# One HGRN2 / forgetting-attention / MoE step: the HGRN rows of w_out multiplied inside decode, the other rows later, by tokens

## The chip, the core and the metric

The kernel runs on one NeuronCore of a Trainium2 chip, in float32 throughout. The time is device microseconds of one execution. The kernel before took 1868.43 us (median of 3 runs, 1866.72 to 1868.97).
## The reference, cut to what matters

```python
def merge_heads(fox_o, hgrn_o, hg, mem_o, g_hn, w_out):
    hgrn_o = rms_norm(hgrn_o, g_hn).reshape(B, L, HGRN_W) * jax.nn.silu(hg)
    cat = concatenate([fox_o (6*128), hgrn_o (6*128), mem_o (4*128)], axis=-1)
    return cat @ w_out                       # w_out 2048 x 2048

# prompt: 256 tokens; sample: 8 batches x 4 tokens, each over 1024 paged keys (8 pages) + 4 new
fox_o = fox_attend(fq, k_all, v_all, c_q, c_k, ...)   # 6 heads
mem_o = memory_attend(mq, mk, mv)                     # 4 heads, 256 memory tokens
h = x + merge_heads(...)
y = h + hier_moe(rms_norm(h), ...)    # group logits (4), expert logits (32), top-2, 32 experts of 512
```

Prompt and sample tokens together are T = 288 (tiles of 128, 128 and 32). The sample's attention (decode) reads per batch 8 key pages and 8 value pages of 384 KB and 512 KB each of memory keys and values. The experts' weights are 403 MB.

## The kernel before

All engines run programs written out by hand in one block; semaphores alone order them. The span has four stages.

1. **Projections, prompt attention, HGRN2** (0 to 583 us), not touched by the change.
2. **Decode** (583 to 752 us). Per batch, TensorE transposes the keys in 14 units of four 128x128 blocks (`key_in`, L2044; 12 units of pages, 2 of memory keys) into PSUM banks, ACT copies the even units out and DVE the odd ones (`key_out`, L1062 and L1447). Four banks (0 to 3) take turns. `decode_scores` (L2061 to L2073) makes scores, maximum and exponential go over ACT and DVE, `probs_in` transposes the probabilities, `decode_values` (L2104 to L2111) multiplies with the value pages, `decode_heads` (L2119, L2120) picks the heads. TensorE's order is a pipeline over batches: the units of batch b+1 are transposed in the loop of batch b, with that batch's small steps between them, then values(b), scores(b+1), heads(b). Value pages lie in two sets of 8 (POOL issues them, one set refilled after each `decode_values`); key pages in one set, each reloaded by SP once its unit is transposed.
3. **w_out and router** (752 to 905 us). For each of 16 blocks of 128 output columns, 16 products with the w_out block [128x128] stationary and `cat` [128x288] moving (L2172) give the block with columns on partitions. ACT copies it, TensorE transposes it back to tokens (`by_token`, L2147), DVE adds it to `h_tok` (L1523), which x was loaded into; TensorE transposes `h_tok` again (`block_transposed`, L2156), DVE multiplies with the norm's gain, `block_logits` (L2161) makes the 36 logits with tokens in the free dimension; at the end three transposes (L2186) turn them. ACT sums squares (L1100). SP loads w_out in 8 slabs of 2 MB into a ring of 3, and x and the router's weights `w_rt` before slab 3.
4. **MoE** (from 905 us). DVE chooses experts (L1541 on), TensorE gathers tokens (L2203) and multiplies four experts side by side, each in 32 columns of the array (L2239, L2280). Eight units of 2 MB of the first pair of groups are loaded ahead; the ring proper starts with the first unit used (`units_used`, SP L659), so it moves with the gather.

## Time and profile before

| | us |
|---|---|
| median of 3 runs | 1868.43 |
| profiled execution, first to last instruction (span) | 1862.4 |
| median less span (what lies around it) | 6.0 |
| DVE ends the gate product (L1437), the last work ahead of decode | 587.95 |
| first `decode_values` | 615.97 |
| last `decode_values` | 742.03 |
| first product of w_out | 752.04 |
| first logits added by DVE (L1541) | 905.36 |
| first gather (L2203) | 915.43 |

The record gives the profiled execution its span alone, so it is set against the median by the difference of the two, 6.0 us. TensorE (PE) is busy 80% of the span, the 16 DMA engines nearly all of the last 940 us. A stage must be read by itself: the rows further down give busy time, TensorE's granted clock (1.00 is 2.4 GHz, 0.50 is 1.2 GHz), DMA share and GB/s of each.

### The profile page before, as it was taken

The page shows a single profiled execution, that of the slowest core. Times are in us where ns is not written, and L with a number is a line of the kernel's source. Part 1 is how long each engine was busy: PE and PEld are TensorE (multiplying, and loading weights), DVE is VectorE, ACT ScalarE, POOL GpSimd, SP SyncE. Part 2 cuts the span into 40 slices and gives each one's busy share as a digit, 9 for nine tenths or more (in the row PEclk, how much of TensorE's full clock was granted, in tenths as well). Part 3 has the DMA queues.
Part 4 walks back from the last instruction along what each step waited for, and adds up shares of the span by engine and source line. Part 5 has one row for each costly group of instructions (what it writes and reads, how often), then busy time and mean ns, then how long its engine had stood idle before and what let it go on. Part 6 is the DMA issues. An engine that isn't in the chain of part 4 may idle for free.

```text
span 1862.4 us, 23477 instructions
## 1 busy us (share of the span) xinstructions
PE 1485.4 (80%) x9493; PEld 884.7 (48%) x9493; DVE 438.5 (24%) x1140; ACT 219.5 (12%) x508; POOL 78.8 (4%) x141
## 2 busy tenths in 40 slices
PE   6999999999998899999867576576765666666746
PEld 5777777776776666777532131221312213122211
DVE  3106664542133333011301101002010020110201
ACT  3000101003323333111300000000000000000000
POOL 1000000220002221000000000000000000000000
PEclk9999999999999999999887788788888887777878
DMA  7444243432444998636399999999999999999996
GB/s 249 131 131 134 69 137 133 133 126 68 132 156 172 370 396 308 211 118 247 160 414 427 428 427 429 428 429 429 429 429 428 429 428 428 428 429 429 427 427 224
DMA packets 130315, 555.09 MB, mean 298 GB/s; under 512 B 13827, under 2 KB 83524, under 8 KB 104836
## 3 DMA queue, kind: packets, MB, share of 16 engines
q1 hardware_dynamic: 121972, 517.82, 69.9%
q0 software_dynamic: 8272, 36.25, 5.4%
q8 instruction: 53, 0.87, 0.2%
q14 instruction: 18, 0.15, 0.0%
HBM read 545.32 MB, written 8.72 MB: 297 GB/s over the span
## 4 chain that ended last, share of the span: by engine, by line
PE 65%; DMA 29%; DVE 3%; SPq 1%; issue 1%; ACT 1%; DVEq 0%; ACTq 0%
PE PS L1720 21%; PE PS L2239 16%; DMA arena<-in_w_up_e_dram 9%; DMA arena<-in_w_down_e_dram 8%; DMA arena<-in_w_gate_e_dram 8%; PE PS L2280 7%; PE PS L2172 7%; DMA arena<-in_cache_mem_k_dram 3%; PE PS L2044 1%; PE PS L1759 1%; PE PS L2104 1%; PE PS L2203 1%; SPq L669 1%; PE PS L2061 1%; PE PS L1811 1%
## 5 line engine op out<-in xcount | busy, mean ns | idle before, releaser
L1720 PE MATMUL PS<-arena 128*128 128x288 f32 (+1 forms) x1728 | 445.2, 407 | 3.0 <-DVE arena L1191 1.1
L2239 PE MATMUL PS<-arena 128*32 128x512 f32 x1792 | 288.7, 727 | 199.0 <-DMA arena<-in_w_up_e_dram 129.7
L1720 PEld LDWEIGHTS PS<-arena 128*128 128x128 f32 x1728 | 322.3, 191 | 96.3 <-issue 20.3
L2239 PEld LDWEIGHTS PS<-arena 128*32 128x32 f32 x1792 | 69.8, 131 | 409.5 <-issue 194.3
L2280 PE MATMUL PS<-arena 128*32 128x512 f32 x872 | 141.4, 731 | 113.9 <-DMA arena<-in_w_down_e_dram 113.9
L2239 PE MATMUL PS<-front,arena 128*32 128x512 f32 x256 | 143.7, 726 | 0.0
L2280 PEld LDWEIGHTS PS<-arena 128*32 128x32 f32 x872 | 37.5, 131 | 211.7 <-issue 124.6
L2172 PE MATMUL PS<-arena 128*128 128x288 f32 x512 | 130.8, 415 | 0.4 <-DVE arena L1483 0.4
L2172 PEld LDWEIGHTS PS<-arena 128*128 128x128 f32 x512 | 97.8, 193 | 32.4 <-issue 5.5
L1646 DVE TENSOR_TENSOR arena<-arena,PS 128x512 f32<-128x512 f32 (+1 forms) x96 | 65.6, 684 | 158.4 <-PE PS L2219 158.4
L1636 DVE TENSOR_TENSOR arena<-arena,PS 128x512 f32<-128x512 f32 x8 | 5.5, 689 | 404.3 <-PE PS L2239 404.3
L2203 PE MATMUL PS<-arena 128*128 128x128 f32 x768 | 94.0, 282 | 1.4 <-DVE arena L1610 1.4
L2203 PEld LDWEIGHTS PS<-arena 128*128 128x128 f32 x768 | 90.4, 197 | 8.5 <-issue 6.7
L2219 PE MATMUL PS<-arena 128*128 128x512 f32 (+1 forms) x192 | 88.4, 603 | 0.0
L2280 PE MATMUL PS<-front,arena 128*32 128x512 f32 x120 | 70.3, 751 | 0.0
L2044 PE MATMUL PS<-ident,arena 128*128 128x128 f32 x448 | 59.0, 283 | 13.4 <-DMA arena<-in_cache_fox_k_dram 6.1
L1641 DVE COPY arena<-PS 128x512 f32<-128x512 f32 x14 | 9.7, 692 | 216.9 <-PE PS L2280 216.9
L2044 PEld LDWEIGHTS PS<-ident,arena 128*128 128x128 f32 x448 | 51.7, 147 | 17.4 <-DMA arena<-in_cache_fox_k_dram 7.4
L2219 PEld LDWEIGHTS PS<-arena 128*128 128x128 f32 (+1 forms) x192 | 29.0, 163 | 58.8 <-issue 46.2
L1130 ACT ACTIVATE arena<-PS 128x512 f32<-128x512 f32 x8 | 4.8, 597 | 341.3 <-PE PS L2266 341.3
L1447 DVE COPY arena<-PS 128x512 f32<-128x512 f32 x56 | 38.1, 686 | 24.7 <-PE PS L2044 24.7
L839 POOL DMA_DIRECT2D arena<-in_cache_fox_v_dram x64 | 34.6, 540 | 215.6 <-issue 215.6
(351 smaller groups left out, 1196.7 us busy)
## 6 DMA issues: line engine op xcount, KB each, us to landing
arena<-in_w_gate_e_dram SPq DMA_DIRECT2D x56, 2048.0 KB, 14.8
arena<-in_w_up_e_dram SPq DMA_DIRECT2D x56, 2048.0 KB, 15.0
arena<-in_w_down_e_dram SPq DMA_DIRECT2D x53, 2048.0 KB, 15.3
arena<-in_cache_fox_k_dram SPq DMA_DIRECT2D x64, 384.0 KB, 8.6
arena<-in_cache_fox_v_dram POOLq DMA_DIRECT2D x64, 384.0 KB, 7.1
arena<-in_w_in_dram SPq DMA_DIRECT2D x6, 3072.0 KB, 10.8
arena<-in_w_out_dram SPq DMA_DIRECT2D x8, 2048.0 KB, 9.2
front<-in_w_gate_e_dram SPq DMA_DIRECT2D x8, 2048.0 KB, 23.3
```

The lines of the kernel that those rows point to most:

```text
L669: sp.dma_start(group_unit(GROUPS - 1, x)[:, D + c * 512:D + (c + 1) * 512], w_down_q[(QUADS - 1) * XQ + x, 3, :, cols]).then_inc(last_in[c ...
L839: pool.dma_start(vpage[par][g], v_pages[ds(page, 1)].rearrange("g t n -> t (g n)")).then_inc(v_in[par], 16)
L1447: dve.tensor_copy(dst, PS[:, key_bank(b, i), :].rearrange("p (h t) -> p h t", h=dst.shape[1])).then_inc(kt_dve, 1)
L1646: dve.tensor_tensor(o, o, PS[0:w, 2 + n % 4, :], ALU.add).then_inc(part_added, 1)
L1720: last = pe.matmul(PS[0:m, bank, 0:w], wt[:, k, c:c + m], rhs[:, k, :], start=(k == 0), stop=(k == KC - 1))
L1759: pe.matmul(PS[:, 6 + j % 2, 0:rhs.shape[1]], ones[:, :], rhs, start=True, stop=True).then_inc(intra_filled, 1)
L2044: last = pe.transpose(PS[:, key_bank(b, i), a * P:(a + 1) * P], src, ident[:, :])
L2172: last = pe.matmul(PS[:, n % 2, 0:T], wo_slot[(n // 2) % 3][:, k, c:c + P], cat[:, k, :], start=(k == 0), stop=(k == KC - 1))
L2203: last = pe.matmul(o, h_scaled[:, t, c * P:(c + 1) * P], pick_tok[:, t, :, :].rearrange("p x s -> p (x s)"), start=(t == 0), stop=(t == 2))
L2219: pe.matmul(PS[0:w, 2 + n % 4, :], gate_slot[:, t0:t0 + w], yslot[:, c * 512:(c + 1) * 512], start=True, stop=True).then_inc(part_filled, 1)
L2239: last = pe.matmul(PS[x * SLOTS:(x + 1) * SLOTS, which, :], xgT[:, kk, x * SLOTS:(x + 1) * SLOTS], wt[:, k, :], start=(kk == 0), stop=(kk ...
L2280: last = pe.matmul(PS[x * SLOTS:(x + 1) * SLOTS, YB[n], :], hT[:, q, x * SLOTS:(x + 1) * SLOTS], wt[:, n * 512:(n + 1) * 512], start=(q == ...
```

## The change

- **HGRN rows in decode.** After every odd key unit TensorE makes one product of HGRN rows for the prompt (`hgrn_prompt`: `cat` block [128 features x 128 tokens] stationary, w_out rows [128x512] moving, result by tokens in bank 2), and after units 1, 5 and 9 also four 32-column products for the sample (`hgrn_sample`, bank 3). Batch b does prompt tile b%2 of column slab b//2. DVE adds the finished tile to `h_tok` (`filler_added`). w_out's HGRN rows come in four slabs of 1.5 MB.
- **Two key banks** (0 and 1) in place of four, since banks 2 and 3 hold w_out sums.
- **Other rows later, by tokens** (`rest_prompt`, `rest_sample`): 10 products per tile, 12 tiles. Two of the tiles are made in the last batch. The transposes back (L2147) and the copies for them are gone. `tile_transposed` and `tile_logits` stand between the products; logits come by tokens, so the last turn (L2186) is gone. The gain is multiplied into `w_rt` once.
- **Value pages** in one ring of 12; POOL loads pages 4 to 7 of batch b+1 after `decode_values(b)`.
- **Loads that move.** Key pages 5, 6, 7 of batch 0 wait for the copy `qk_new` (new; `gate_done` 2), as do TensorE's first key units. x is loaded by SP ahead of batch 1's keys. Router biases and `w_rt` are issued by POOL after the last `decode_heads`; TensorE waits for them (`rt_in`) before its next product.

```diff
+        K_EARLY = 5
+        kpage = [view(RAW + 4096, FW), view(RAW + FV * T, FW), view(RAW + FV * T + FW, FW), front[:, 0:FW], front[:, 1504:1504 + FW]] + \
+                [view(RAW + 4096 + g * FW, FW) for g in (1, 2, 3)]
+        VRING = 12
+        vring = [view(WORK + s * FW, FW) for s in range(VRING)]
+
...
+        qk_new = view(RAW, 16, NS)
...
-            return (2 * b + i) % 4
+            return i % 2
...
-            for g in range(6):
+            def load_wo_hgrn(n):
+                sp.dma_start(wo_hgrn[n % 2], w_out_d[:, 6:12, n * 512:(n + 1) * 512]).then_inc(wo_in[n % 2], 16)
+
+            def load_wo_rest(n, landed):
+                sp.dma_start(wo_rest[n][:, 0:HF, :], w_out_d[:, 0:HF, n * 512:(n + 1) * 512]).then_inc(landed, 16)
+                sp.dma_start(wo_rest[n][:, HF:HF + HM, :], w_out_d[:, 12:16, n * 512:(n + 1) * 512]).then_inc(landed, 16)
+
+            for g in range(K_EARLY):
                 load_key_page(0, g, True)
-            sp.wait_ge(hn_sum, len(SUMS))
-            for g in (6, 7):
-                load_key_page(0, g, True)
+            load_wo_hgrn(0)
             sp.wait_ge(pa_out, NU)
             load_mem_keys(0, True)
...
+            sp.wait_ge(gate_done, 2)
+            for g in range(K_EARLY, NPG):
...
             sp.wait_ge(out_done, 16 * no)
             for t, (t0, n) in enumerate(TILES):
                 sp.dma_start(h_tok[0:n, t, :], x_tok_d[t]).then_inc(x_again, 16)
-            sp.dma_start(b_rt[:, 0:NG], b_router_group).then_inc(rt_in, 16)
-            sp.dma_start(b_rt[:, NG:NG + NE], b_router_expert).then_inc(rt_in, 16)
-            sp.dma_start(w_rt[:, :, 0:NG], w_rg_d).then_inc(rt_in, 16)
-            sp.dma_start(w_rt[:, :, NG:NG + NE], w_re_d).then_inc(rt_in, 16)
-            for n in range(3, 8):
-                sp.wait_ge(wo_filled, 2 * (n - 2))
-                sp.dma_start(wo_slot[n % 3], w_out_d[:, :, n * 256:(n + 1) * 256]).then_inc(wo_in[n % 3], 16)
+            for g in range(4):
+                load_key_page(1, g)
+            load_wo_hgrn(1)
+            for g in range(4, NPG):
+                load_key_page(1, g)
+            load_mem_keys(1)
+            for b in range(2, NB):
+                for g in range(NPG):
+                    load_key_page(b, g)
+                load_mem_keys(b)
+                if b in (4, 6):
+                    sp.wait_ge(fill_done, b - 2)
+                    load_wo_hgrn(b // 2)
+
+
+            sp.wait_ge(kt_filled, NB * KU)
+            sp.wait_ge(fill_done, 6)
+            load_wo_rest(0, wo_in[2])
+            sp.wait_ge(d_scored, NB)
+            load_wo_rest(1, wo_in[0])
+            sp.wait_ge(d_pv, NB)
+            load_wo_rest(2, wo_in[1])
...
-            for x in range(2):
-                load_first(0, x)
+            load_first(0, 2)
             load_first(1, 3)
-            sp.wait_ge(wo_filled, 12)
-            load_first(0, 2)
-            sp.wait_ge(wo_filled, 14)
+            sp.wait_ge(d_ot, NB)
+            sp.wait_ge(fill_done, NB)
+            load_first(0, 1)
+            sp.wait_ge(wo_filled, 3)
+            load_first(0, 0)
             load_first(0, 3)
-            sp.wait_ge(h_added, 3 * KC)
+            sp.wait_ge(wo_filled, 6)
+            load_wo_rest(3, wo_in[2])
+            sp.wait_ge(wo_filled, NWO)
...
+            def load_values(b, g):
+                used = NPG * b + g - VRING
+                if used >= 0 and (g == 0 or used % NPG == 0):
+                    pool.wait_ge(d_pv, used // NPG + 1)
+                page = pool.value_load(ptab_row[0:1, ds(b * NPG + g, 1)], min_val=0, max_val=POOL - 1)
+                pool.dma_start(vpage(b, g), v_pages[ds(page, 1)].rearrange("g t n -> t (g n)")).then_inc(v_in[b % 2], 16)
...
+            pool.wait_ge(d_pv, NB)
+            pool.wait_ge(d_ot, NB)
+            pool.dma_start(b_rt[:, 0:NG], b_router_group).then_inc(rt_in, 16)
+            pool.dma_start(b_rt[:, NG:NG + NE], b_router_expert).then_inc(rt_in, 16)
+            pool.dma_start(w_rt[:, :, 0:NG], w_rg_d).then_inc(rt_in, 16)
+            pool.dma_start(w_rt[:, :, NG:NG + NE], w_re_d).then_inc(rt_in, 16)
+
+            pool.wait_ge(wo_filled, 9)
...
+            dve.wait_ge(pa_out, NU)
+            dve.tensor_copy(qk_new[:, 0:2 * HF, :], raw[:, FQ:FQ + 2 * HF, SEQ:T])
+            dve.tensor_copy(qk_new[:, 2 * HF:2 * HF + HM, :], raw[:, MQ:MQ + HM, SEQ:T]).then_inc(gate_done, 1)
+            dve.wait_ge(gate_done, 2)
+            dve.wait_ge(out_done, 16 * N_ROWS_OUT)
...
+            def filler_added(b):
+                n, t = divmod(b, 2)
+                o = h_tok[:, t, n * 512:(n + 1) * 512]
+                if b == 0:
+                    dve.wait_ge(x_again, 48)
+                dve.wait_ge(fill_done, b + 1)
+                if t:
+                    for j in range(4):
+                        s = h_tok[0:NS, 2, n * 512 + j * P:n * 512 + (j + 1) * P]
+                        dve.tensor_tensor(s, s, PS[32 * j:32 * j + 32, 3, n * P:(n + 1) * P], ALU.add)
+                dve.tensor_tensor(o, o, PS[:, 2, :], ALU.add).then_inc(fill_added, 1)
...
+            dve.wait_ge(rt_in, 64)
+            dve.tensor_tensor(w_rt, w_rt, G_FFN.rearrange("p (k a) -> p k a", a=1).to_broadcast([P, KC, NG + NE]), ALU.mult).then_inc(gate_done, 1)
+            dve.wait_ge(bias_filled, 1)
+            dve.tensor_copy(b_all, PS[:, 2, 64:64 + NG + NE])
...
-                if b or i >= 4:
-                    pe.wait_ge((kt_act, kt_dve)[i % 2], b * (KU // 2) + (i // 2 - 1))
+                if b or i >= 2:
+                    pe.wait_ge((kt_act, kt_dve)[i % 2], b * (KU // 2) + i // 2)
...
+            def hgrn_prompt(b, k):
+                n, t = divmod(b, 2)
+                if k == 0:
+                    pe.wait_ge(wo_in[n % 2], 16 * (n // 2 + 1))
+                    if b:
+                        pe.wait_ge(fill_added, b)
+                last = pe.matmul(PS[:, 2, :], cat[:, 6 + k, t * P:(t + 1) * P], wo_hgrn[n % 2][:, k, :], start=(k == 0), stop=(k == HG - 1))
+                if k == HG - 1:
+                    last.then_inc(fill_done, 1)
+
+            def hgrn_sample(b, k):
+                n = b // 2
+                for j in range(4):
+                    pe.matmul(PS[strip(j), 3, n * P:(n + 1) * P], cat[:, 6 + k, SEQ:T], wo_hgrn[n % 2][:, k, j * P:(j + 1) * P],
+                              start=(k == 0), stop=(k == HG - 1))
+
+            def filler(b, i):
+                if i % 2 and i < 12:
+                    hgrn_prompt(b, i // 2)
+                if i in (1, 5, 9):
+                    hgrn_sample(b, 3 * (b % 2) + i // 4)
...
+            def rest_prompt(n, t, ks):
+                for k in ks:
+                    if t == 0 and k == 0:
+                        pe.wait_ge(*WO_IN[n])
+                    if n and k == 0:
+                        pe.wait_ge(h_added, WO_TILES.index((n - 1, t)) + 1)
+                    last = pe.matmul(PS[:, t, :], cat[:, WO_K[k], t * P:(t + 1) * P], wo_rest[n][:, k, :],
+                                     start=(k == 0), stop=(k == HF + HM - 1))
+                    if k == HF + HM - 1:
+                        last.then_inc(wo_filled, 1)
+
+            def rest_sample(n):
+                pe.wait_ge(*WO_IN[n])
+                if n:
+                    pe.wait_ge(h_added, WO_TILES.index((n - 1, 2)) + 1)
+                for k in range(HF + HM):
+                    for j in range(4):
+                        last = pe.matmul(PS[strip(j), 3, n * P:(n + 1) * P], cat[:, WO_K[k], SEQ:T], wo_rest[n][:, k, j * P:(j + 1) * P],
+                                         start=(k == 0), stop=(k == HF + HM - 1))
+                last.then_inc(wo_filled, 1)
+
+            def tile_transposed(m):
+                n, t = WO_TILES[m]
+                w = TILES[t][1]
+                pe.wait_ge(h_added, m + 1)
+                if m >= 2:
+                    pe.wait_ge(ht_drained, m - 1)
+                for c in range(4):
+                    last = pe.transpose(PS[:, 5 + m % 2, c * w:(c + 1) * w], h_tok[0:w, t, n * 512 + c * P:n * 512 + (c + 1) * P], ident[0:w, 0:w])
+                last.then_inc(ht_filled, 1)
+
...
+            def tile_logits(m):
+                pe.wait_ge(ht_drained, m + 1)
...
+                for c in range(4):
+                    last = pe.matmul(logits_ps[t][0:w], hT_blk[m % 2][:, c * w:(c + 1) * w], w_rt[:, 4 * n + c, :],
+                                     start=(n == 0 and c == 0), stop=(n == 3 and c == 3))
+                last.then_inc(lg_filled, 1)
+
+            pe.wait_ge(gate_done, 2)
...
+                    filler(b, i)
+                    if b + 1 == NB and i < HF + HM:
+                        rest_prompt(0, 0, (i,))
                 decode_values(b)
                 if b + 1 < NB:
                     decode_scores(b + 1)
+                else:
+                    rest_prompt(0, 1, range(HF + HM))
...
+            pe.wait_ge(rt_in, 64)
+            pe.wait_ge(fill_added, NB)
+            pe.matmul(PS[:, 2, 64:64 + NG + NE], ones[0:1, :], b_rt, start=True, stop=True).then_inc(bias_filled, 1)
+            def advance(m):
+                tile_transposed(m)
+                if m:
+                    tile_logits(m - 1)
+
+            pe.wait_ge(moe_prep, 1)
+            rest_sample(0)
+            advance(0)
+            for n in range(1, 4):
+                rest_sample(n)
+                advance((1, 5, 8)[n - 1])
+                for t in range(2):
+                    rest_prompt(n, t, range(5))
+                    advance(((2, 4), (6, 7), (9, 10))[n - 1][t])
+                    rest_prompt(n, t, range(5, HF + HM))
+                    if (n, t) in ((1, 0), (3, 1)):
+                        advance(3 if n == 1 else 11)
+            tile_logits(NWO - 1)
```

What stands on TensorE in one round of the key units in the decode loop, before (L2044 key transposes with the waits for the copies out of the bank; `tok_in` and `k_in` are the page semaphores; L2078 turns the maxima):

```order
L2044 MATMUL PS<-ident,arena 128x128 [waits kt_act,tok_in0]
L2044 MATMUL PS<-ident,arena 128x128 x3
L2044 MATMUL PS<-ident,arena 128x128 [waits kt_dve,tok_in1]
L2044 MATMUL PS<-ident,arena 128x128 x3
L2044 MATMUL PS<-ident,arena 128x128 [waits kt_act,tok_in1,tok_in0]
L2044 MATMUL PS<-ident,arena 128x128 x3
L2078 MATMUL PS<-ident,part_max 1x128 [waits d_max]
```

and now (L2087 the same transposes, L2172 and L2179 the prompt's and the sample's HGRN products):

```order
L2087 MATMUL PS<-ident,arena 128x128 [waits kt_act,tok_in0]
L2087 MATMUL PS<-ident,arena 128x128 x3
L2087 MATMUL PS<-ident,arena 128x128 [waits kt_dve,tok_in1]
L2087 MATMUL PS<-ident,arena 128x128 x3
L2172 MATMUL PS<-arena 128x512 [waits fill_added,wo_in0]
L2179 MATMUL PS<-arena 32x128 x4
L2087 MATMUL PS<-ident,arena 128x128 [waits kt_act,tok_in1,tok_in0]
L2087 MATMUL PS<-ident,arena 128x128 x3
L2121 MATMUL PS<-ident,part_max 1x128 [waits d_max]
```

The products stand behind each odd unit; the unit after them waits for the copy of the unit two before it, where it was four before.

Where the w_out stage begins on TensorE, before (L2120 the end of `decode_heads`, L2172 products of a block, L2147 transposes back, L2176 the bias row):

```order
L2120 MATMUL PS<-mix,arena 128x16
L2172 MATMUL PS<-arena 128x288 [waits wo_in0,d_out]
L2172 MATMUL PS<-arena 128x288 x15
L2172 MATMUL PS<-arena 128x288 [waits wo_in0]
L2172 MATMUL PS<-arena 128x288 x15
L2147 MATMUL PS<-ident,arena 128x128 [waits wo_drained]
L2147 MATMUL PS<-ident,arena 128x128
L2147 MATMUL PS<-ident,arena 32x128
L2172 MATMUL PS<-arena 128x288 [waits wo_drained,wo_in1]
L2172 MATMUL PS<-arena 128x288 x15
L2176 MATMUL PS<-arena,ones 128x36 [waits rt_in]
```

and now (L2196 rest rows of the prompt, L2162 and L2163 `decode_heads` of the last batch, L2259 the bias row, L2207 rest rows of the sample, L2218 transposes, L2228 logits):

```order
L2196 MATMUL PS<-arena 128x512 x10
L2162 MATMUL PS<-mix,arena 128x4 [waits d_rcp,d_oc]
L2162 MATMUL PS<-mix,arena 128x4 x5
L2163 MATMUL PS<-mix,arena 128x16
L2259 MATMUL PS<-arena,ones 128x36 [waits fill_added,rt_in]
L2207 MATMUL PS<-arena 32x128 [waits wo_in2,moe_prep]
L2207 MATMUL PS<-arena 32x128 x39
L2218 MATMUL PS<-ident,arena 128x128 [waits h_added]
L2218 MATMUL PS<-ident,arena 128x128 x3
L2207 MATMUL PS<-arena 32x128 [waits h_added,wo_in0]
```

and on POOL, at the end of its program:

```order
L871 DMA arena<-in_cache_fox_v_dram 128x768
L888 DMA arena<-in_b_router_group_dram 1x4x1 [waits d_ot,d_pv]
L889 DMA arena<-in_b_router_expert_dram 1x16x2
L890 DMA arena<-in_w_router_group_dram 128x16x4
L891 DMA arena<-in_w_router_expert_dram 128x16x32
```

The bias product, which waited for `rt_in` behind three blocks of products, now stands right behind `decode_heads`, and the four loads that it waits for are issued only when `decode_heads` is done.

## Rows read from the trace of the kernel before

**Rows 1.** Page, busy tenths in 40 slices of the span.
```profile
PE   6999999999998899999867576576765666666746
PEclk9999999999999999999887788788888887777878
DMA  7444243432444998636399999999999999999996
```
**Rows 2.** Windows by stage: stretch, length, busy per engine, PEclk, DMA share, GB/s.
```profile
580.00:755.00 175.00, 156.57 (x1795) 110.96 (x1794) 62.82 (x172) 55.86 (x109) 40.26 (x72) 0.93 0.89 334
755.00:900.00 145.00, 145.00 (x621) 108.24 (x620) 15.52 (x59) 21.10 (x97) 0.30 (x1) 0.99 0.54 188
900.00:924.00 24.00, 15.24 (x88) 12.44 (x90) 14.85 (x74) 15.52 (x24) 1.50 (x1) 0.72 0.66 263
924.00:1862.00 938.00, 616.24 (x4064) 230.41 (x4064) 110.80 (x195) 30.41 (x48) 0.00 (x0) 0.82 0.98 414
```
**Rows 3.** Chain that ended last, in decode: start us, us, what.
```profile
596.26 18.57 DMA arena<-in_cache_mem_k_dram
...
615.97 2.72 PE PS L2104 x32
...
619.81 2.59 PE PS L2061 x48
...
624.40 1.43 PE PS L2119 x12
...
628.73 2.77 PE PS L2044 x24
...
633.54 2.72 PE PS L2104 x32
...
636.80 0.57 PE PS L2111 x16
...
726.63 2.72 PE PS L2104 x32
```
**Rows 4.** Windows at the start of decode (columns as in rows 2).
```profile
580.00:600.00 20.00, 15.37 (x168) 12.00 (x167) 8.07 (x15) 8.17 (x12) 8.22 (x15) 1.00 0.82 294
600.00:615.00 15.00, 8.43 (x48) 6.50 (x47) 5.13 (x14) 5.59 (x11) 1.15 (x3) 0.77 1.02 398
```
**Rows 5.** Groups of instructions in decode: the copies out of the key banks.
```profile
L1447 DVE COPY arena<-PS 128x512 f32<-128x512 f32 x56 | 38.1, 686 | 24.7 <-PE PS L2044 24.7
L1062 ACT ACTIVATE arena<-PS 128x512 f32<-128x512 f32 x56 | 33.3, 597 | 68.1 <-PE PS L2044 67.5
```
**Rows 6.** Chain from the w_out stage to the experts.
```profile
770.86 7.76 PE PS L2172 x32
...
891.23 7.97 PE PS L2172 x32
...
903.52 1.28 ACT L1114
...
905.36 0.58 DVE arena L1541 x3
...
915.43 8.45 PE PS L2203 x48
...
923.99 7.00 PE PS L2239 x64
931.00 5.56 PE PS L2203 x48
```
**Rows 7.** Loads issued by POOL, 1024 pieces of 512 bytes each: issue ns, landing.
```profile
L812 POOL DMA_DIRECT2D arena<-in_state_hgrn_dram x4: 887/887/887, 339.8 to 384.8; - x4
...
DMA to landing us min/median/max: 4.5/4.7/5.9
```
**Rows 8.** Timeline of SP: its issue of w_rt's expert columns.
```profile
762.79 10.94 SPq L651 DMA_DIRECT2D arena<-in_w_router_expert_dram  x1
```
**Rows 9.** Window while w_rt's small pieces move (columns as in rows 2).
```profile
771.00:772.00 1.00, 1.00 (x6) 0.79 (x5) 0.00 (x0) 0.00 (x0) 0.00 (x0) 1.00 0.96 51
```

More of the change, by code:

```diff
@@ L234, in build @@
         ahead = view(YT + KC * P, UNIT)
-        w_rt = view(FREE, KC, NG + NE)
-        xgain = view(FREE + KC * (NG + NE), 2, T)
+        w_rt = view(WORK + 14592, KC, NG + NE)
+        hT_blk = [view(WORK + 14592 + KC * (NG + NE) + n * 512, 512) for n in range(2)]
         gate_slot = view(FREE + 2 * FB * P, T)
@@ L281, in build @@
         assert NPART == len(GPARTS)
+        WO_TILES = [(n, t) for n in range(4) for t in ((0, 1, 2) if n == 0 else (2, 0, 1))]
+        NWO = len(WO_TILES)
+        WO_K = [k for k in range(KC) if not 6 <= k < 12]
         HTF = [(t, c, 4) for t in range(2) for c in range(0, KC, 4)] + [(2, 0, KC)]
@@ L321, in build @@
         PS = ctx.enter_context(nc.psum_tensor("PS", [P, 8, 512], f32))
+        logits_ps = [PS[:, n, 0:NG + NE] for n in (4, 7, 2)]
         consts_set = sem("consts_set")
@@ L2066, in decode_scores @@
                 for h in range(HF):
-                    pe.matmul(new, q_fox[:, 32 * h:32 * h + 32], raw[:, FK + h, SEQ:T], start=(h == 0), stop=False)
+                    pe.matmul(new, q_fox[:, 32 * h:32 * h + 32], qk_new[:, HF + h, :], start=(h == 0), stop=False)
                 pe.matmul(new, sel_b, decay[:, PAST:KEYS], start=False, stop=False)
@@ L2138, in _ @@
                     decode_scores(b + 1)
+                else:
+                    rest_prompt(0, 1, range(HF + HM))
                 decode_heads(b)
[L2142 to L2148 removed]
@@ L2150, in block_transposed @@
-            def block_transposed(n):
-                pe.wait_ge(h_added, 3 * n + 3)
-                if n >= 2:
-                    pe.wait_ge(ht_drained, n - 1)
-                for t, (t0, w) in enumerate(TILES):
-                    last = pe.transpose(PS[:, 5 + n % 2, t0:t0 + w], h_tok[0:w, t, n * P:(n + 1) * P], ident[0:w, 0:w])
-                last.then_inc(ht_filled, 1)
-            def block_logits(n):
-                pe.wait_ge(ht_drained, n + 1)
-                last = pe.matmul(PS[0:NG + NE, 4, 0:T], w_rt[:, n, :], xgain[:, n % 2, :], start=(n == 0), stop=(n == KC - 1))
-                last.then_inc(lg_filled, 1)
```

188 lines of the change are left out of this document (67 added, 121 removed).

## The prediction

> **What bounds the kernel now.** I read the page's slices first, then the windows by stage, then the chain of waits inside decode and around its two ends. The slices show TensorE full up to the middle of the span and the DMA engines full behind it [rows 1]. From 924 us on the DMA share is 0.98 at 414 GB/s and TensorE is busy two thirds of the time [rows 2]: the experts' weights stream, and that stream's length is set by bytes. It starts with the first unit used, so the change is worth what it moves the first gather (915.43 us) and the first expert products (923.99 us) [rows 6]. Before that, w_out (755 to 900 us) has TensorE busy in every microsecond at clock 0.99 and the DMA at 0.54: bound by TensorE. Decode (580 to 755 us) has both near their limits, TensorE 156.6 of 175 us, DMA 0.89 [rows 2].
>
> Inside decode the chain gives the price of a batch. From the values of batch 0 to those of batch 1 it runs 615.97 to 633.54 us, 17.57 us, without leaving TensorE. The six batches to 726.63 us average 18.44 us, so DMA waits cost 0.9 us a batch [rows 3]. Ahead of them is the one long wait: the memory keys of batch 1 are issued at 596.26 us and land 18.57 us later, behind everything queued; the DMA share is 1.02 there, at 398 GB/s, and TensorE's clock falls to a mean of 0.77 [rows 3, 4]. So decode has little room: about 8 us at its start and 5 us after. What is put into it beyond that lengthens it.
>
> **The work that moves.** The trace shows no product with 512 moving columns and a full 128x128 stationary block on its own. The nearest are the experts' quads, 32 products of 512 columns, four side by side, in 7.00 us, thus 0.875 us per 512 columns [rows 6], and w_out's own blocks, 16 products of 288 columns in 7.76 to 7.97 us, 0.49 us each or 1.70 ns a column [rows 6], which gives 0.871 us for 512. I take 0.871; the ends, 0.85 and 0.90, would move the 128 prompt products by 3 us either way. A sample quad (four 128-column products side by side) takes 0.285 us: L2111, two quads, 0.57 us [rows 3]. All w_out then costs 128 x 0.871 + 64 x 0.285 = 129.7 us, against 256 x 0.49 = 125 to 127 us: the products get no cheaper by turning them. The gain must come from filled waits and from the transposes.
>
> One rule speaks against the quads. The Trainium skill, TensorE: Matmul & The Clock Gate, section "Wait — 56ns, not 53.3ns?", has the sequencer spend about 62 ns per matmul, which binds when the array's work is shorter. A quad is eight instructions, 0.50 us by that rule, which would add 14 us over 64 quads; but the row above has 16 of them in 0.57 us, 36 ns each, so I go by the row.
>
> **Step 1, start of decode.** Ahead of batch 1's memory keys there now stand three more key pages (5 to 7 of batch 0, 1.18 MB, late because of the wait for `qk_new`), x (2.36 MB) and a w_out slab (1.57 MB), and four value pages fewer (-1.57 MB): +3.54 MB. At 398 GB/s [rows 4] that is 8.9 us, so the keys land at 623.7 and the first values start 1.1 us behind them, at 624.8 us. The other bound: if the transfer is not what is late, TensorE is. It starts at about 589 (DVE ends its gate product at 587.95 and makes two copies), makes 14 units on two banks (a pair costs 0.46 us of transposes, four of L2044's 115 ns [rows 3], 0.69 us of copy [rows 5] and some 0.3 us of handing over: 1.45 us; 7 pairs 10.2, last copy 0.9), scores 4.6, and the next loop of 13.9 us (step 2: 7.5 of the 17.57 plus 6.5): 618.6 us. I take the DMA bound, since the DMA was what ended last there before. The six HGRN products of batch 0 (6.1 us with their quads) are hidden in this wait.
>
> **Step 2, six batches.** A period is 17.57 + 6 x 0.871 + 3 x 0.285 = 23.65 us. Two banks: after an odd unit the product (0.87 or 1.16 us) covers the copies (0.60 on ACT, 0.69 on DVE [rows 5]), since pair and product take 1.8 us against the 1.45 above. Not covered is unit 13, which waits for DVE's copy of unit 11, behind the 1.2 us of `probs_out` and sums: 0.4 us. So 24.05 us. DVE's `filler_added` (0.7 us, every second batch 1.6) stands behind the last copy and ahead of the next maximum, while TensorE has values and scores to do (8 us): nothing. DMA per batch is 7.3 MB and at most 1.6 MB of slab, 22 us at 400 GB/s: no longer the bound; the 12-page ring gives pages 4 to 7 a full period to arrive. 624.8 + 6 x 24.05 = 769.1 us for the values of batch 6.
>
> **Step 3, last batch.** Values 3.8, scores 4.6 and heads 1.7 are 10.1 us (from the chain's starts at 615.97, 619.81 and 624.40 us [rows 3]), small steps 1.2, HGRN 6.1, ten rest products 8.7: 26.1. Slab 0 of the rest (2.6 MB) is issued when the last key unit is filled, needed 10 us later and shares the engines with four value pages; 6.6 us alone, some 11 shared: 1 us. Values at 796.2; they take 3.8, then ten products 8.7, heads 1.7: 810.4 us.
>
> **Step 4, the new wait.** Here TensorE waits for `rt_in`. Before, w_rt was loaded under the second and third block and cost nothing. Now POOL issues four loads after `decode_heads` and TensorE has nothing in front of the wait. POOL's issue of 1024 pieces takes 0.89 us and they land 4.5 to 4.7 us after it began [rows 7]. w_rt is 2 x 2048 pieces: two small issues 1.2, two large 1.25 each, then the pieces. Before, they moved at 51 GB/s in a window of share 0.96 [rows 9], about 3.5 us in all, behind an SP issue that took 10.94 us in a full queue [rows 8]. Now 6 to 9 MB of w_out and expert units are in the SP queue beside them. 3.7 of issue, some 3.3 of pieces, 2 of completion (what the 4.7 leave after 0.9 of issue and the move itself): 9 us, so TensorE resumes at 819.4. Bounds: 5 us (one 4.7 us landing from the first large issue, all else under it) and 16 us (they land only when the SP backlog does). After such an idle TensorE restarts at the lower level, 1.2 GHz: the gather at 915.43, behind 1.4 us of waiting and little work before it, took 8.45 us where the same work later took 5.56 [rows 6]. I add 2.8 us.
>
> **Step 5, the rest.** 60 prompt products 52.3, 40 quads 11.4, 12 x 4 transposes at 0.115 5.5, logits 12 x 4 x 2 x 0.119 (L2119: 12 in 1.43 us [rows 3]) less the narrow sample tiles 9.6, less 2.4 of them behind the last product: 76.4, plus 0.8 where the sample's second slab waits for DVE's first three additions. The last product ends at 819.4 + 2.8 + 77.2 = 899.4; before it was 899.2. Behind it: addition 0.9, transposes 0.6, copy and square on ACT 1.5, root and reciprocal 0.8: 3.8 us, against 6.2 before, where ACT worked off its small squares and loaded a table for 1.28 us [rows 6]. The logits' first addition is at 903.2 us. Everything behind it is as before.
>
> Sum against before, stretch by stretch: to the first values +8.8 (624.8 for 615.97 us); six batches +33.6 (144.3 for 110.7); from there to the end of the last heads +15.9 (41.3 for 25.4, 726.63 to 752.04 us); the new wait and its clock +11.8; products and logits of w_out -70.0 (77.2 for 147.2, 752.04 to 899.2 us); the tail -2.4. Together -2.3 us, or 903.1 for 905.36 us. For the profiled execution that is a span of 1860.1 us, and with the 6.0 us by which the median of the runs lies above its span, 1866.1 us. A difference under 0.2% (3.7 us) is no change that this measurement can tell. The likeliest case is just that; its own range is 1860 to 1872.
>
> **Rivals.**
> A. *The new waits are shorter.* The start of decode is bound by TensorE (values at 618 to 621 instead of 624.8, -4 to -7 us), or w_rt lands in 5 us and the clock stays up (-4 to -7). For it: the 18.57 us wait before held pages that were not urgent. Against: DMA share 1.02 [rows 4]. With one of them 1861 us, with both 1855. The Trainium skill, DMA: Bandwidth & Descriptors, section "Anatomy of one DMA — SWDGE (gpsimd) path", gives 2.0 us plus bytes over 436 GB/s for a load from POOL, thus an estimate of 2.6 us for the 256 KB of w_rt, and calls descriptor generation small: that would be this rival's lower wait. No row here has 128-byte pieces from POOL.
> B. *Two banks stall TensorE in every batch (slower).* Place: the units behind `strips_max`, the exponentials (1.3 us on ACT) and `probs_out`. Price: up to 0.5 us more at each of three places, 1.2 us in 7 batches, +8.4 us: 1874.6. It decides from a period of 25 us on. For it: four banks hid all of this before, and TensorE waits in program order. Against: a product of 0.87 us behind each pair.
> C. *w_rt crawls beside the SP queue (slower).* Six megabytes still queued at 400 GB/s are 15 us; small pieces that take turns with large ones land when these do: +7 us, 1873.
>
> **Chances.** Forecast 0.42, A 0.30, B 0.16, C 0.12. The forecast's own range reaches over both borders: 0.11 of it faster, 0.29 same, 0.02 slower. A: 0.27 faster, 0.03 same; B: 0.15 slower; C: 0.08 slower, 0.04 same, with 0.01 of B. Faster 0.38, same 0.37, slower 0.25. For 8 in 10 the range takes all of B and C and A down to one of its two waits nearly gone and half the other: 1856 to 1879; a period or a product off by its bounds (3 us) is in it.
>
> **What would show it.** First values at 625 (618: rival A); period of values 24 us (25 or more: B); TensorE idle between the last L2163 and L2259 9 us and the clock at 0.5 behind it (5: A, 15: C); the product L2196 at 0.87 us; first logits at 903; the stretch from there to the end 957 us as before. I am wrong if the expert stream gets longer or shorter by itself, or if a slab of w_out lands late.

## The result

The changed kernel takes 1882.38 us (median of 4 runs, 1881.3 to 1883.37); beside it the kernel before took 1868.70 us (4 runs, 1866.72 to 1870.87). The ratio is 1.0082, 95% interval 1.0062 to 1.0102: slower by 11.6 to 19.1 us. The prediction was 1866.1 us, no change, with a range to 1879: wrong in sign and outside its range. A later comparison (after_again) gave 1.0077 (1.0052 to 1.0101).

The stretches, from the traces of one execution each (a second trace of the same changed kernel, after_again, has its first values at 631.2 us and its gather 3.1 us earlier, so a stretch of one trace can be off by 2 to 3 us):

| | before | predicted | after |
|---|---|---|---|
| first values | 615.97 | 624.8 | 633.36 |
| six batches | 110.7 | 144.3 | 150.9 |
| from there to the last heads' end | 25.4 | 41.3 | 44.1 |
| wait for the router's weights | none | 9.0 | 14.9 |
| from there to the last product's end | 147.2 | 80.0 (clock 2.8 in it) | 77.1 |
| tail to the first logits | 6.2 | 3.8 | 3.4 |
| first logits | 905.36 | 903.2 | 923.82 |
| from there to the end | 957.0 | 957.0 | 957.9 |
| span | 1862.4 | 1860.1 | 1881.7 |

### The profile page after: what moved, and what is told of

The parts are those of the page before. It is cut to its first block, busy times and chain, and to the rows that moved or that the text cites. A ratio compares the mean times of both kernels' runs of the same rounds, so it can differ in the third digit from the quotient of the medians.

```text
span 1881.7 us, 23700 instructions
## 1 busy us (share of the span) xinstructions
PE 1487.6 (79%) x9762; PEld 845.7 (45%) x9762; DVE 443.0 (24%) x1126; ACT 209.3 (11%) x433; POOL 81.3 (4%) x144
## 4 chain that ended last, share of the span: by engine, by line
PE 65%; DMA 28%; DVE 4%; issue 1%; SPq 1%; ACT 1%; POOL 0%; DVEq 0%; ACTq 0%; POOLq 0%
PE PS L1763 21%; PE PS L2329 16%; DMA arena<-in_w_up_e_dram 9%; DMA arena<-in_w_down_e_dram 9%; DMA arena<-in_w_gate_e_dram 8%; PE PS L2370 7%; PE PS L2196 4%; PE PS L2087 2%; PE PS L2172 2%; PE PS L1802 1%; DMA arena<-in_cache_fox_k_dram 1%; PE PS L2147 1%; PE PS L2104 1%; PE PS L2293 1%; PE PS L2309 1%
## 5 line engine op out<-in xcount | busy, mean ns | idle before, releaser
L1763 PEld LDWEIGHTS PS<-arena 128*128 128x128 f32 x1728 | 322.3, 191 | 96.2 <-issue 20.3
L2293 PEld LDWEIGHTS PS<-arena 128*128 128x128 f32 x768 | 90.0, 196 | 8.5 <-issue 6.7
L2196 PE MATMUL PS<-arena 128*128 128x512 f32 x160 | 74.1, 608 | 1.3 <-DMA arena<-in_w_out_dram 1.3
L2087 PE MATMUL PS<-ident,arena 128*128 128x128 f32 x352 | 61.0, 301 | 14.2 <-DMA arena<-in_cache_fox_k_dram 6.6
L2087 PEld LDWEIGHTS PS<-ident,arena 128*128 128x128 f32 x352 | 44.9, 155 | 28.1 <-issue 19.4
L2172 PE MATMUL PS<-arena 128*128 128x512 f32 x96 | 52.5, 630 | 0.0
L1098 ACT ACTIVATE arena<-PS 128x512 f32<-128x512 f32 x56 | 33.5, 597 | 122.1 <-PE PS L2087 122.1
L2196 PEld LDWEIGHTS PS<-arena 128*128 128x128 f32 x160 | 29.2, 191 | 32.8 <-issue 31.3
```

Of the source, the lines that this page charges most:

```text
L1098: act.activation(dst, PS[:, key_bank(b, i), :].rearrange("p (h t) -> p h t", h=dst.shape[1]), ACT.Copy).then_inc(kt_act, 1)
L1763: last = pe.matmul(PS[0:m, bank, 0:w], wt[:, k, c:c + m], rhs[:, k, :], start=(k == 0), stop=(k == KC - 1))
L2087: last = pe.transpose(PS[:, key_bank(b, i), a * P:(a + 1) * P], src, ident[:, :])
L2172: last = pe.matmul(PS[:, 2, :], cat[:, 6 + k, t * P:(t + 1) * P], wo_hgrn[n % 2][:, k, :], start=(k == 0), stop=(k == HG - 1))
L2196: last = pe.matmul(PS[:, t, :], cat[:, WO_K[k], t * P:(t + 1) * P], wo_rest[n][:, k, :], start=(k == 0), stop=(k == HF + HM - 1))
L2293: last = pe.matmul(o, h_scaled[:, t, c * P:(c + 1) * P], pick_tok[:, t, :, :].rearrange("p x s -> p (x s)"), start=(t == 0), stop=(t == 2))
```

## The profile after

The page's slices, against [rows 1]. A slice is 47 us: TensorE dips in the 13th (564 to 611 us, the start of decode; 7 tenths for 8) and in the 18th (800 to 847 us; 6 for 9, no dip before).

```profile
PE   6999999999997999969875766657666676666746
PEclk9999999999997999989888887888878788787868
DMA  7444243432535999763389999999999999999996
```

Windows by stage (stretch, length, busy per engine, PEclk, DMA share, GB/s), against [rows 2, 4]:

```profile
580.00:600.00 20.00, 11.29 (x53) 8.44 (x51) 5.45 (x9) 6.52 (x9) 7.24 (x13) 0.77 0.70 239
600.00:620.00 20.00, 14.89 (x124) 8.49 (x124) 3.72 (x8) 1.88 (x4) 0.00 (x0) 0.67 1.02 359
620.00:785.00 165.00, 163.60 (x1648) 100.06 (x1644) 59.29 (x159) 44.82 (x90) 30.28 (x54) 0.97 0.85 304
785.00:830.00 45.00, 42.10 (x308) 19.87 (x300) 5.74 (x23) 4.75 (x9) 3.92 (x7) 0.96 0.69 256
830.00:843.20 13.20, 0.00 (x0) 0.00 (x0) 0.00 (x0) 0.00 (x0) 2.43 (x3) 0.50 1.00 351
843.20:921.00 77.80, 76.30 (x566) 43.28 (x566) 10.61 (x26) 11.96 (x33) 1.81 (x1) 0.98 0.25 94
921.00:942.00 21.00, 13.05 (x85) 12.66 (x85) 12.28 (x66) 12.28 (x10) 0.00 (x0) 0.67 0.76 301
942.00:1881.00 939.00, 614.70 (x4065) 230.63 (x4064) 110.86 (x195) 30.42 (x48) 0.00 (x0) 0.82 0.98 414
```

The last row is that of before, 18 us later: the experts' stream has the same length and rate. All the loss lies ahead of it. From 620 to 785 us TensorE is busy 163.6 of 165 us, at 0.97: no room is left there. In the fifth row no engine computes for 13.2 us; only GpSimd issues its loads.

The chain of waits (start us, us, what), for [rows 3, 6]; the lines up to 645.59 us are the start and the first batch:

```profile
597.53 19.95 DMA arena<-in_cache_fox_k_dram
...
633.36 2.72 PE PS L2147 x32
...
643.45 0.92 PE PS L2087 x8
644.37 0.86 PE PS L2172 x2
645.23 0.36 PE PS L2179 x8
645.59 0.59 PE PS L2087 x4
...
784.70 10.83 DMA arena<-in_w_out_dram
...
814.26 2.72 PE PS L2147 x32
818.11 8.78 PE PS L2196 x20
831.24 11.98 DMA arena<-in_w_router_expert_dram
843.90 3.83 PE PS L2207 x80
...
933.89 8.06 PE PS L2293 x48
942.07 3.12 PE PS L2329 x25
```

Three DMAs stand on the chain: a key page of batch 1, the first slab of the rest, and `w_rt`. In [rows 3] the first of them was the memory keys, which stand last in a batch. Now TensorE waits for memory keys nowhere in decode. An HGRN product takes 0.86 us and ten rest products (20 rows) 8.78 us, for the 0.871 predicted; a key unit alone takes 0.59 us (0.46).

## The experiments

Each edit is of the changed kernel, or of the kernel before where that is said. Parentheses in an edit stand for the lines that they name. "Gather" is the first gather's start in the profiled execution: 915.43 us before, 933.89 after (930.78 in after_again).

### The router's weights early

```diff
-        w_rt = view(WORK + 14592, KC, NG + NE)      # + b_rt, hT_blk, sq_out placed around it
+        w_rt = view(WORK + 16128, KC, NG + NE)
-            pool.wait_ge(d_pv, NB); pool.wait_ge(d_ot, NB); (four loads)
             for b in range(NB):
+                if b == 4: (the four loads)
```

> Edit: the router weights and biases get columns that are free during decode and are loaded by GpSimd ahead of batch 4's value pages, in the place of the loads behind the last heads. Theory (the router wait is a pure loss, 14.9 us between the last heads and L2259, plus 4 x (3.83 - 2.35 us) of products at half clock behind it): no wait behind the last heads, L2259 at about 829, the first sample quads at full clock or nearly, the first logits 15 to 17 us earlier, 1865 to 1868 us. Rival 1 (the wait only hid the slabs of w_out behind it: slab 1 and 2, issued at 814 to 818 us, land late then): under 8 us of gain, and a wait for DMA ahead of the rest's second block. Rival 2 (what the DMA engines don't move while TensorE waits they must move later, in the expert stream): first logits 15 us earlier, but the stretch behind them longer by as much, 1880 or so.

1868.33 us (10 runs), 1.0009 of before (0.9997 to 1.0021): 14 us faster than the changed kernel. TensorE's timeline goes from the last heads to the bias (L2258 here) without a gap, and the first ten sample quads behind it take 2.43 us in the place of 3.83:

```profile
829.65 0.37 PE L2162 MATMUL PS<-mix,arena 128*128 128x16 f32 x2
829.96 0.41 PE L2258 MATMUL PS<-arena,ones 1*128 1x36 f32 x2
```

The gather starts at 919.33 us, 14.6 earlier (the first logits too, for 15 to 17 expected; the last batch was 2.2 us longer in this trace), and the end follows it. Both rivals are out: no slab is late behind it, and the stream does not lengthen.

### Nothing beside the router's loads

```diff
             sp.wait_ge(d_pv, NB)
+            sp.wait_ge(rt_in, 64)
             load_wo_rest(2, wo_in[1])
```

> Edit: SyncE waits for the router's loads to land before it issues the rest's slab 2 and the first expert units, so that the small pieces have the engines nearly for themselves (slab 1 alone stands beside them); nothing else moves. Crowding theory (the prediction's case C: the small pieces take turns with 2 MB units): the wait for rt_in falls from 14.9 us to 7 to 9 us, the first logits come 6 to 8 us earlier, about 1875 us, if slab 2 and the expert units still come in time. Rival (the small pieces and GpSimd's issue are what costs, whatever stands beside them): the wait stays at 12 us or more and the time at 1879 to 1885 us.

1876.53 us (4 runs), 1.0057 (1.0035 to 1.0079). Loads in flight around the wait, changed kernel first, then this one (KB each, median us from issue to landing):

```profile
arena<-in_w_gate_e_dram SPq DMA_DIRECT2D x1, 2048.0 KB, 16.7
arena<-in_w_router_expert_dram POOLq DMA_DIRECT2D x1, 256.0 KB, 12.0
```

```profile
arena<-in_w_router_expert_dram POOLq DMA_DIRECT2D x1, 256.0 KB, 4.4
```

The waits of TensorE (us in total, times, longest) in the two kernels:

```profile
PE PS L2259 <- DMA arena<-in_w_router_expert_dram: 14.9, 1, 14.9
```

```profile
PE PS L2260 <- DMA arena<-in_w_router_expert_dram: 7.3, 1, 7.3
```

In this kernel nothing else moves then: from 830 to 838 us the DMA share is 0.27, for 1.00 in the changed kernel. So 7.6 us of the wait are crowding by slab 2 and the expert units, and 7.3 us are GpSimd's issue and the loads themselves. The crowding theory held for the wait. The first logits came 5.1 us earlier (918.70 for 923.82), not 6 to 8: the last batch was 2.2 us longer in this trace, and the first ten quads took 4.47 us for 3.83.

### x behind batch 1's keys

```diff
-            (x into h_tok); load_key_page(1, 0..3); load_wo_hgrn(1); load_key_page(1, 4..7); load_mem_keys(1)
+            load_key_page(1, 0..7); load_mem_keys(1); (x into h_tok); load_wo_hgrn(1)
```

> Edit: x and the second HGRN slab of w_out (together 3.9 MB) are issued behind batch 1's key pages and memory keys, ahead of batch 2's, in the place of ahead of and amid batch 1's key pages. Theory (batch 0's loop waits for batch 1's first key page, which stands behind x in the queue): that page lands 6 to 9 us earlier than 617.5, the first values come at 625 to 628 in the place of 633.4 us, and 1874 to 1876 us. Rival (the engines are full there, and the 3.9 MB only move on: batch 2's keys are late by as much in batch 1's loop, or DVE waits for x ahead of its first addition): first values earlier, second values not, and the time within 2 us of the changed kernel's 1882.

1880.07 us (4 runs), 1.0071 (1.0046 to 1.0096). First values at 627.68 us, 5.7 earlier than in the changed kernel's trace; the gather is 4.0 earlier, since one more period took 26.2 us. The medians show only 2.3 us, less than expected. Part of that is the draw: six other traces with an unchanged start have their first values at 631.0 to 633.1 us, so x later is worth 3.3 to 5.7 us. The 3.9 MB were not late elsewhere: the second period's length is the clock's (below), and no wait for x or keys follows.

What is left of the start shows in the chain of this run:

```profile
606.00 5.05 PE PS L2102 x48
...
613.05 1.02 PE PS L2085 x8
...
627.68 2.72 PE PS L2145 x32
```

Batch 0's scores end at 613 us and the loop follows at once, 14.6 us without a wait for a load. But 613 us is late. TensorE's first key units start at 589 us, wait three times for batch 0's own key pages (4.3 us in all), and then it runs at half clock: 48 rows of scores take 5.05 us here and 2.59 in a later batch.

### The first rest slab in two parts

```diff
-            sp.wait_ge(kt_filled, NB * KU)
             sp.wait_ge(fill_done, 6)
-            load_wo_rest(0, wo_in[2])
+            (rows 0:6 of slab 0) -> wo_in[2]
+            sp.wait_ge(kt_filled, NB * KU)
+            (rows 12:16 of slab 0) -> rest_in, waited for at the seventh product
```

> Edit: the first slab of the rest is loaded in its two parts on their own semaphores, its first six rows issued behind batch 7's memory keys (their place is free since batch 5's products), its last four as before when the last key unit is filled; the products wait for each part at their own row. Theory (in the last batch TensorE waits for the slab, issued at 784.7 and landed at 795.5, and runs at half clock behind it): values of batch 7 follow those of batch 6 by 26 to 27 us in the place of 30.0, and 1877 to 1879 us. Rival (the last batch is long for the product count and the clock falls without the wait): 29 to 30 us between them, and no change in the time within 1.5 us.

1880.2 us (4 runs), 1.0079 (1.0057 to 1.0101). The last values follow those of batch 6 by 26.9 us (the chain: 781.82 to 808.75) in the place of 30.0, and the wait for w_out is gone. (In the other traces with these loads and the heads at this place the stretch is 29.1, 29.9, 32.2 and 32.2 us.)

```profile
781.82 2.72 PE PS L2149 x32
785.67 2.59 PE PS L2106 x48
808.75 2.72 PE PS L2149 x32
```

The local effect is the expected one, worth 2.1 to 5.3 us against these five traces; the medians show 2.2 us.

### The heads moved

In two of the six periods the changed kernel needs 26.2 us in the place of 24.6. Windows of one of them: the clock falls right behind the heads' products (L2162 and L2163, the last starting at 692.31 us), with TensorE busy all the time; a mean of 0.66 over 5 us is 3.4 us at half clock, and it costs 1.6 us. All seven traces of the changed kernel and its variants with the heads at this place (42 periods) show 16 such falls, each within 1 us of the heads' end.

```profile
690.00:692.00 2.00, 2.00 (x31) 1.49 (x28) 0.91 (x4) 0.00 (x0) 1.08 (x2) 1.00 1.07 405
692.00:697.00 5.00, 5.00 (x31) 3.09 (x31) 0.73 (x2) 0.60 (x1) 2.16 (x4) 0.66 1.02 405
697.00:709.00 12.00, 11.80 (x84) 7.60 (x86) 5.58 (x16) 4.92 (x11) 0.00 (x0) 1.00 0.91 320
```

```diff
                     filler(b, i)
+                    if b and i == 1:
+                        decode_heads(b - 1)
...
                 else:
                     rest_prompt(0, 1, range(HF + HM))
-                decode_heads(b)
+                    decode_heads(b)
```

> Edit: of the changed kernel, the head products (14 of 4 or 16 columns) of a batch move from behind the scores into the next batch's loop, behind the first HGRN product. In the changed kernel two of six periods are 26.2 us in the place of 24.6, with TensorE at half clock for some 5 us behind the heads. Theory (the stretch of small products ahead of it is what lets the clock fall): no period of 26.2 us, all 24.6 or less, 2 to 4 us saved, 1878 to 1880 us. Rival 1 (the clock falls for a reason outside this order): again one to three periods of 26 us, the half-clock stretch at another place, and 1881 to 1883 us. Rival 2 (the heads now stand in the way of the key copies' hand-over and fill a wait on the banks): periods of 24.0 us.

1882.83 us (4 runs), 1.0089 (1.0073 to 1.0104): no gain, although all six periods of the trace were 24.6 us. So it was run again beside the changed kernel:

> The changed kernel itself once more, as the standard for the next run on the same chip. Expected: 1882 us, periods of 24.6 us with one to three of 26.2, first values at 631 to 633 us.

> The changed kernel with the moved heads once more (all its periods were 24.6 us in the trace, yet its four runs had the median of the changed kernel). Theory (the move keeps the clock up in decode; what it gives is partly lost in the wait for the rest's first slab behind it, 3.2 us for 1.3): no period above 25 us again and 1 to 3 us below after_again. Rival (the move does nothing, the clean periods were luck): periods of 26 us again and a ratio of the two medians within 0.05% of 1.

The changed kernel: 1882.71 us (6 runs), periods 24.6 with two of 26.2. With moved heads: 1882.04 (6 runs), six periods of 24.6 again, clock 1.00 over all of them. But the last values came 35.8 us behind those of batch 6, for 29.1 in after_again. TensorE's granted clock there:

```profile
783.00:790.00 7.00, 4.35 (x82) 2.22 (x74) 0.79 (x2) 0.75 (x1) 2.88 (x5) 0.92 1.04 397
790.00:796.00 6.00, 5.79 (x19) 2.88 (x20) 0.00 (x0) 0.00 (x0) 0.00 (x0) 0.50 1.02 389
796.00:802.00 6.00, 6.00 (x14) 3.34 (x15) 0.68 (x1) 0.00 (x0) 0.00 (x0) 0.50 0.64 238
```

Both sides were half right. The move keeps the clock up in decode (3 us). The wait for the slab is 2.9 us, for 0.3 in after_again and 1.3 in the changed kernel's first trace (the heads' 1.7 us no longer stand ahead of it), with more half clock behind it, which takes the gain back. What the order does shows only once that wait is gone, in the combination.

### The combinations

> Edit: the early router loads, x and the second HGRN slab behind batch 1's keys, and the first rest slab in two parts, all three together; nothing else differs from the changed kernel. Theory (the three waits are independent losses and add up): first expert products 5.7 + 14.3 + 3 = 23 us earlier than the changed kernel's 942.0 us, at about 919, against 923.9 before the change; span about 1859 us, a time of 1859 to 1863 us, thus 0.2 to 0.4% faster than before the change. Rival (the waits hide each other: TensorE arrives earlier at slabs 1 and 2, which the DMA engines can't bring earlier): waits for w_out in the rest stage of 4 us or more, and a time of 1866 us or above.

1862.09 us (9 runs), 0.9975 (0.9964 to 0.9987): faster than before. Gather at 911.57 us, no wait for w_out. The three edits nearly add up: 22.3 us at the gather, for 24.3 alone (14.6, 4.0 and 5.7), with one fall of the clock more than in the changed kernel.

> Edit: the three of combo and the moved heads. Expected: combo's time, less 2 to 4 us if the moved heads keep the clock up (1856 to 1860 us), the same as combo's (1859 to 1863 us) if they don't.

1854.36 us (5 runs), 0.9935 (0.9922 to 0.9949). Gather at 905.02 us. Windows (start, six batches, last batch, rest, tail): the clock is 1.00 from 627 to 893 us.

```profile
580.00:627.00 47.00, 34.93 (x257) 23.00 (x259) 14.36 (x31) 14.57 (x24) 7.22 (x13) 0.82 0.94 327
627.00:775.00 148.00, 146.80 (x1552) 89.91 (x1554) 53.60 (x145) 38.59 (x78) 33.66 (x58) 1.00 0.92 328
775.00:816.00 41.00, 41.00 (x314) 19.78 (x306) 5.91 (x22) 4.75 (x9) 2.88 (x5) 1.00 0.63 228
816.00:893.00 77.00, 75.04 (x572) 42.30 (x572) 10.89 (x29) 11.99 (x34) 1.80 (x1) 1.00 0.41 162
893.00:913.00 20.00, 12.19 (x79) 11.81 (x78) 12.20 (x65) 12.25 (x10) 0.00 (x0) 0.66 0.73 305
```

Against combo, 7.7 us, more than the 2 to 4 expected: 5.0 us by the last heads (three periods of 26.2 us became 24.6), 1.6 more by the first quads of the rest, which combo ran at half clock (4.00 us for ten) and this one at full (2.43). That is 6.6 us at the gather; the other 1.1 us of the medians no trace explains.

### The heads moved in the kernel before

> Edit: the kernel before with the heads moved in the same way, into the next batch's loop behind its second key unit; nothing else. It tells how much of combo_heads' gain has nothing to do with the change. Theory (the clock falls behind scores and heads in before, too: periods of 18.8, 20.8 and 18.4 us for 17.6): periods of 17.6 us except where a key page is late, 2 to 5 us faster than before, 1862 to 1865 us. Rival (there the periods above 17.6 us are waits for key pages, which only move): within 1 us of before.

1866.36 us (12 runs), 0.9989 (0.9972 to 1.0005): within the error of nothing. Its periods still reach 21.5 and 22.2 us, and TensorE's waits are for keys, 12.7 us in all (9.6 before), so the rival holds in the main. The combination's gain is not one that the kernel before could have had this way.

```profile
PE PS L2044 <- DMA arena<-in_cache_mem_k_dram: 6.4, 3, 2.9
PE PS L2044 <- DMA arena<-in_cache_fox_k_dram: 6.3, 5, 2.0
```

The theory was not empty, though: in the trace of before one of the six periods (20.8 us) has such a fall, at the end of the heads and with TensorE busy, so it does not come with the HGRN products. With the heads moved none of the six has a fall while TensorE is busy.

```profile
662.00:665.00 3.00, 3.00 (x16) 3.00 (x16) 0.36 (x1) 0.60 (x1) 1.59 (x3) 0.50 1.04 399
```

### Two banks in the kernel before

```diff
-            return (2 * b + i) % 4
+            return i % 2
...
-                if b or i >= 4:
-                    pe.wait_ge((kt_act, kt_dve)[i % 2], b * (KU // 2) + (i // 2 - 1))
+                if b or i >= 2:
+                    pe.wait_ge((kt_act, kt_dve)[i % 2], b * (KU // 2) + i // 2)
```

> Edit: the kernel before with two PSUM banks for the keys in the place of four, the waits on the copies one turn tighter; nothing else. It prices the banks alone, without a product between the pairs. My sum: a pair of key units costs 0.46 + 0.69 + 0.3 = 1.45 us in the place of 0.92, so 7 x 0.53 = 3.7 us a batch, of which the DMA waits of before (0.9 us) hide a part: periods of 21 us, 17 to 22 us in all, 1885 to 1890 us. Rival (the copies hide behind the other unit's transposes and the small steps): periods of 18.5 us and less than 4 us in all. The difference to the changed kernel's period (24.6 less 6.1 of products is 18.5) then says how much of the banks' price the products cover.

1887.88 us (4 runs), 1.0109 (1.0082 to 1.0136). The medians differ by 21.3 us, as summed. Its shortest period is 21.07 us (642.11 to 663.18), 3.5 above 17.57. The chain shows the pair as it was summed, copy, hand-over, unit:

```profile
656.49 0.70 DVE arena L1447
657.19 0.14 issue
657.33 0.64 PE PS L2044 x4
```

In the changed kernel the products take 6 x 0.86 + 3 x 0.36 = 6.24 us, and the period less these (24.62 - 6.24) is 18.38 us, 0.8 above 17.57. So the HGRN products, put between the pairs, cover 2.7 of the banks' 3.5 us. This prices the banks without products; within the changed kernel it is an inference from the two periods.

### Four value pages later

```diff
                 for g in range(NPG):
+                    if (b, g) == (1, 0):
+                        pool.wait_ge(kt_filled, KU)
                     load_values(b, g)
```

> Edit: combo_heads, and GpSimd issues the first four value pages of batch 1 (1.57 MB, which stand beside batch 0's last key pages and batch 1's first) only when batch 0's key units are filled. Theory (the start is bound by the DMA engines: three waits for key pages, 4.7 us in all, and the page behind batch 0's scores): first values 2 to 4 us earlier than 626.9, 1850 to 1852 us. Rival (the pages that are waited for are bound by their late issue at 589 us and the half clock behind each wait, not by the share of the engines): first values within 1 us of 626.9 and 1854 us.

1855.28 us (6 runs), 0.9932 (0.9909 to 0.9956); first values at 627.5 us. The theory fell: with 1.57 MB less, the waits for batch 0's key pages are 5.1 us for 4.7. What would shorten the start further was not found.

## Why the prediction was wrong

The mechanism of TensorE's work was right: a product 0.86 to 0.88 us, the rest stage 77.1 us with its half clock for 80.0. The expert stream followed the gather as said. The slab's wait and the router's were placed where they came, and came out too cheap; the wait at the start was placed at the wrong load. No shorter wait of rival A came.

- **Step 1, the start: +8.6 us.** The step that failed is "the six HGRN products of batch 0 (6.1 us with their quads) are hidden in this wait". The wait was read from before, where the keys of batch 1 flow in and only the memory keys, last in the loop, are late. After the change x (2.36 MB) stands ahead of batch 1's *first* pages, the second of which lands at 617.5 us; the whole loop, products and all (15.8 us), comes behind it, and the memory keys are not waited for at all. A wait at a loop's head hides nothing of the loop. x_later gives 3.3 to 5.7 us back. The other bound failed too: TensorE alone was to have first values at 618.6 us, and x_later, which waits for no load behind batch 0's scores, has them at 627.7. That sum had no wait for batch 0's own late pages (4.3 us there) and no half clock.
- **Step 2, six batches: +6.6 us**, 0.57 a period (24.62 for 24.05) and 3.2 for two falls of the clock, a term that was not in the sum at all. The period's miss is 0.2 us of quads (0.36 each behind a product, for 0.285) and, for the rest, the two banks, 0.8 us for 0.4: lone units at 0.59 us for 0.46, a pair at 1.02 for 0.92, the last unit behind DVE's sums. Rival B's price, 1.2 us a batch, was not reached.
- **Step 3, last batch: +2.8 us.** The slab landed 10.8 us after its issue, as said (11), and the wait was 1.3 us for 1. What was missed is the half clock behind it; slab_split gives 3.1 us back against this trace.
- **Step 4, the router's wait: +5.9 us.** The 9 us left 1.7 us for the crowd above the unhindered 7.3, and the crowd cost 7.6: rival C, which stood as the upper bound of 16 us and got 0.12. The estimate from the Trainium skill's formula (DMA: Bandwidth & Descriptors, "Anatomy of one DMA — SWDGE (gpsimd) path") was 2.6 us for this load: measured 4.4 us with little beside it, 12.0 us in the crowd.
- **Step 5 and tail: -3.3 us**, since quads cost 0.24 us (L2207, 80 rows in 2.39 us) and not 0.285, and the half clock 1.5 us and not 2.8. The Trainium skill's 62 ns (TensorE: Matmul & The Clock Gate, "Wait — 56ns, not 53.3ns?") is stated there for hardware decode switched off, and no run here shows whether it is. Per row of the trace it does not fit: 80 rows in 2.39 us are 30 ns a row. Per float32 product, two rows, the 60 ns come near it, but so does the price by columns: 0.86 us for 512 are 0.215 us for the 128 of a quad. What sets the quad's pace stays open.
- **A product of 512 columns.** The prediction says that the trace of before has none on a full block alone. It has, at L2219 in the experts' stage (12 rows in 5.42 us, 0.90 us a product), which is the prediction's own upper bound; nothing hung on it.
- **The span against the median.** The 6.0 us "around the span" were not that: every profiled run here has a time 1.6 to 1.7 us above its span (1883.37 for 1881.7). By that, the execution of before that was profiled was itself some 4.5 us faster than its median, that of the changed kernel 1.0 slower; single executions of before go from 1862 to 1877 us. So the spans differ by 19.3 us where the medians differ by 13.7. This error offset 5.3 us of the 21.6 by which the span was missed, which leaves 16.3 by the medians.

Where the gain went: three loads came to stand behind new waits or made one, which cost 3.3 to 5.7 us (x), 2.1 to 5.3 us (slab) and 14.6 us (router, at the gather). With these mended the same division of work is 4.5 us faster than before by the medians, and with the heads moved 12.3 us.

## What to carry to other kernels

When a load is moved, ask which *first* consumer waits behind it, not which was last late; only work that stands ahead of that consumer in its engine's program is hidden. Small loads issued when the big queue has just been refilled land with it: load them a stage earlier, into columns that are free. When a local gain does not show in the time, look for the next wait behind it and remove both before judging either.

## What was not expected of the hardware

- TensorE's clock fell from 2.4 to 1.2 GHz for 3.4 us while it was busy without a gap, in 16 of 42 periods and in one of the six of the kernel before, each time at the end of the scores and the 14 head products of 4 or 16 moving columns. In 24 periods of four traces with the heads behind a 512-column product it never fell. Which property of that stretch decides is open.
- 256 KB in 128-byte pieces from GpSimd landed in 4.4 us with the engines nearly idle (share 0.27), and in 12.0 us beside a slab and expert units of 2 MB.
- The expert stream from the first expert products on took 938 to 940 us in every kernel here, wherever from 913 to 945 us it began; the 13 us in which nothing was computed gave nothing back later.
